# w_down in two transfers of 2 MB, and an up projection on interleaved pairs of columns

## What is computed

```
logits = v @ w_router + b_router            # 32 experts, the best 4 for each token
for each expert e, with the tokens that chose it:
    h   = x @ w_up[e] + b_up[e]             # 1024 -> 2048
    glu = min(h[:, :1024], 7)
    lin = clip(h[:, 1024:], -7, 7)
    act = glu * sigmoid(1.702 * glu) * (lin + 1)
    y   = act @ w_down[e] + b_down[e]       # 1024 -> 1024
f = sum over a token's 4 experts of gate * y
```

## Time and profile before

| | |
|---|---|
| three timed runs | 1293.08, 1294.69, 1295.81 us; median 1294.69 |
| the profiled execution | 1289.3 us, of which the span (first to last instruction) is 1287.5 |
| TensorE busy | 1198.5 us, 93% of the span |
| w_up matmuls (L909) | 2240 instructions, 504.7 us busy, mean 596 ns |
| w_down matmuls (L943) | 1120 instructions, 250.7 us busy, mean 601 ns |
| VectorE, ScalarE, GpSimd busy | 44%, 20%, 12% |
| SyncE's DMA queue | 52809 packets, 460.11 MB, 87.0% of 16 engines' span |
| chain that ended last | 63% TensorE, 26% transfers, 8% VectorE |

### The profile page before, as it was taken

How to read it: one execution, slowest core, us unless ns; L and a number is a source line. 1 busy time by engine, 2 the same in 40 slices (tenths; PEclk the granted TensorE clock), 3 DMA queues, 4 the chain that set the end, 5 groups by cost and what they waited for, 6 DMA issues and landing times.

```text
span 1287.5 us, 17057 instructions
## 1 busy us (share of the span) xinstructions
PE 1198.5 (93%) x5960; PEld 517.8 (40%) x5961; DVE 563.7 (44%) x1059; ACT 255.8 (20%) x404; POOL 160.7 (12%) x96
## 2 busy tenths in 40 slices
PE   5999999979999999899999999999999999999991
PEld 2688885523333333333333333333333333333330
DVE  0507815774443443344433444433444434434457
ACT  1523210242112111111112111212111211111121
POOL 0556462045200000000000000000000000000024
PEclk9999999989999999999999999999999999999995
DMA  9966696469999999999987999997999999699961
GB/s 334 349 248 263 247 301 227 145 257 419 406 427 427 427 426 426 425 426 426 428 379 300 427 425 428 426 428 303 377 427 427 428 426 426 262 424 426 427 252 41
DMA packets 54780, 466.33 MB, mean 362 GB/s; under 512 B 5511, under 2 KB 5671, under 8 KB 18633
## 3 DMA queue, kind: packets, MB, share of 16 engines
q1 hardware_dynamic: 52809, 460.11, 87.0%
q0 software_dynamic: 1952, 5.97, 1.4%
HBM read 464.29 MB, written 1.77 MB: 362 GB/s over the span
## 4 chain that ended last, share of the span: by engine, by line
PE 63%; DMA 26%; DVE 8%; ACT 1%; POOL 1%; issue 1%; SPq 0%; DVEq 0%; ACTq 0%; POOLq 0%
PE bank L909 26%; DMA ring<-in_w_up 24%; PE bank L943 12%; PE bank L695 8%; PE bank L885 3%; PE bank L746 3%; PE bank L763 2%; DMA ring<-in_w_ada 2%; PE bank L810 2%; PE bank L637 1%; PE bank L681 1%; PE bank L934 1%; DVE front L1407 1%; POOL front L547 1%; ACT front L1100 1%
## 5 line engine op out<-in xcount | busy, mean ns | idle before, releaser
L909 PE MATMUL bank<-ring,front 128*64 128x512 f32 x2240 | 504.7, 596 | 21.0 <-DMA ring<-in_w_up 21.0
L909 PEld LDWEIGHTS bank<-ring,front 128*64 128x64 f32 x2240 | 152.8, 137 | 314.4 <-issue 268.8
L943 PE MATMUL bank<-ring,front 128*64 128x512 f32 x1120 | 250.7, 601 | 6.8 <-ACT front L1100 6.8
L1380 DVE TENSOR_TENSOR front<-front,bank 128x512 f32<-128x512 f32 (+1 forms) x210 | 143.9, 685 | 56.8 <-PE bank L885 35.1
L1366 DVE TENSOR_TENSOR O_parts<-bank,O_parts 64x512 fp32r<-64x512 f32 x70 | 48.2, 689 | 239.2 <-ACT O_parts L1066 234.7
L943 PEld LDWEIGHTS bank<-ring,front 128*64 128x64 f32 x1120 | 77.9, 138 | 155.8 <-issue 142.0
L1097 ACT ACTIVATE front<-front 128x256 f32<-128x256 f32 x70 | 29.2, 417 | 504.3 <-DVE front L1398 504.3
L579 POOL TENSOR_TENSOR parts_home<-front 128x1024 f32<-128x1024 f32 (+1 forms) x2 | 5.2, 2576 | 917.8 <-DVE onehot_T L1421 917.8
L1398 DVE TENSOR_SCALAR front<-bank 128x256 f32<-128x256 f32 x70 | 29.7, 425 | 163.7 <-PE bank L909 162.5
L885 PE MATMUL bank<-O_parts,onehot_T 128*128 128x512 f32 x216 | 81.3, 454 | 11.2 <-DVE front L1446 6.5
L1066 ACT ACTIVATE O_parts<-bank 64x512 fp32r<-64x512 f32 x70 | 41.4, 591 | 237.5 <-PE bank L943 236.7
(11 more groups left out here) (217 smaller groups left out, 871.5 us busy)
## 6 DMA issues: line engine op xcount, KB each, us to landing
ring<-in_w_up SPq DMA_DIRECT2D x128, 2048.0 KB, 18.2
ring<-in_w_down SPq DMA_DIRECT2D x128, 1024.0 KB, 17.5
ring<-in_w_ada SPq DMA_DIRECT2D x12, 2048.0 KB, 11.9
ring<-in_w_in SPq DMA_DIRECT2D x7, 2048.0 KB, 8.0
ring<-in_w_o SPq DMA_DIRECT2D x2, 2048.0 KB, 21.0
hx<-in_x_prompt SPq DMA_DIRECT2D x2, 1024.0 KB, 8.2
ring<-in_w_in SPq DMA_DIRECT2D x4, 512.0 KB, 22.3
ring<-in_w_out_a SPq DMA_DIRECT2D x1, 2048.0 KB, 7.6
```

What stands on the lines that cost most here:

```text
L909: last = mm(bank[B_UP[j]][64 * h:64 * h + 64, :], x_T[:, (c % 2) * 2 + b, 64 * (c // 2):64 * (c // 2) + 64], w[:, :, at:at + 256], start=F ...
L943: last = mm(bank[B_DOWN][64 * h:64 * h + 64, :], act_T[:, 2 * j + b, 64 * hh:64 * hh + 64], expert_chunk_at(UP_CHUNKS + m)[:, b * 1024 + h ...
L1380: signal(TT(Y[0:r, 2 * t + h, :], Y[0:r, 2 * t + h, :], bank[b][0:r, :], ALU.add), bank_free[b], value)
```

## The change

w_down comes in two transfers of 2 MB, one for each slot (`DOWN_CHUNKS` 2): four rows of w_down to a partition, 16 KB in one run. Slot j then has row j*512 + 4p + b at place b of partition p, b from 0 to 3. So that `act_T` still meets the right rows, the up projection hands its columns out in another way: half h of group j now has the columns j*512 + 4q + 2h + {0, 1}, q from 0 to 127, for glu and for lin. The new function `columns` selects them, for the weights and for the bias: two neighbours, a gap of two, two neighbours. VectorE's and ScalarE's code stays as it is.

```diff
-UP_CHUNKS, DOWN_CHUNKS = 4, 4
+UP_CHUNKS, DOWN_CHUNKS = 4, 2
 
         def expert_chunk_at(c):
-            if c < UP_CHUNKS:
-                return ring[:, EXPERT_SLOT[c], :]
-            s, half = divmod(c - UP_CHUNKS, 2)
-            return ring[:, EXPERT_SLOT[UP_CHUNKS + s], half * 2048:(half + 1) * 2048]
+            return ring[:, EXPERT_SLOT[c], :]
...
+            def columns(row, j, h):
+                return row.rearrange("p (g j q b) -> p g j q b", g=2, j=2, b=4)[:, :, j, :, 2 * h:2 * h + 2]
...
                     for h in range(2):
-                        at = j * 512 + h * 256
-                        mm(bank[b][64 * h:64 * h + 64, :], up_sel[:, 0:SLOTS],
-                           b_up_parts.rearrange("p (g m) -> p g m", g=2)[:, :, at:at + 256], start=True, stop=False)
+                        mm(bank[b][64 * h:64 * h + 64, :], up_sel[:, 0:SLOTS], columns(b_up_parts, j, h), start=True, stop=False)
...
-                    w = expert_chunk_at(c)[:, b * 2048:(b + 1) * 2048].rearrange("p (g m) -> p g m", g=2)
+                    w = expert_chunk_at(c)[:, b * 2048:(b + 1) * 2048]
                     for h in range(2):
-                        at = j * 512 + h * 256
                         last = mm(bank[B_UP[j]][64 * h:64 * h + 64, :], x_T[:, (c % 2) * 2 + b, 64 * (c // 2):64 * (c // 2) + 64],
-                                  w[:, :, at:at + 256], start=False, stop=c == UP_CHUNKS - 1 and b == 1)
+                                  columns(w, j, h), start=False, stop=c == UP_CHUNKS - 1 and b == 1)
...
-                for m in range(DOWN_CHUNKS):
-                    j, hh = divmod(m, 2)
-                    pe.wait_ge(expert_landed[UP_CHUNKS + m], e * 16 + 16)
-                    for b in range(2):
+                for j in range(DOWN_CHUNKS):
+                    pe.wait_ge(expert_landed[UP_CHUNKS + j], e * 16 + 16)
+                    for b in range(4):
+                        hh = b // 2
                         for h in range(2):
-                            last = mm(bank[B_DOWN][64 * h:64 * h + 64, :], act_T[:, 2 * j + b, 64 * hh:64 * hh + 64],
-                                      expert_chunk_at(UP_CHUNKS + m)[:, b * 1024 + h * 512:b * 1024 + (h + 1) * 512],
-                                      start=m == 0 and b == 0, stop=m == DOWN_CHUNKS - 1 and b == 1)
-                    if m < DOWN_CHUNKS - 1:
-                        last.then_inc(expert_used[UP_CHUNKS + m], 1)
+                            last = mm(bank[B_DOWN][64 * h:64 * h + 64, :], act_T[:, 2 * j + b % 2, 64 * hh:64 * hh + 64],
+                                      expert_chunk_at(UP_CHUNKS + j)[:, b * 1024 + h * 512:b * 1024 + (h + 1) * 512],
+                                      start=j == 0 and b == 0, stop=j == DOWN_CHUNKS - 1 and b == 3)
+                    if j < DOWN_CHUNKS - 1:
+                        last.then_inc(expert_used[UP_CHUNKS + j], 1)
```

More of the change, by code:

```diff
@@ L470, in _ @@
             for c in range(EXPERT_CHUNKS):
-                s = EXPERT_SLOT[c if c < UP_CHUNKS else UP_CHUNKS + (c - UP_CHUNKS) // 2]
+                s = EXPERT_SLOT[c]
                 if s in ROW_SLOT:
```

## The result

| | before | after |
|---|---|---|
| median of the timed runs, us | 1293.08 (7 runs, 1291.88 to 1295.81) | 1298.96 (7 runs, 1296.66 to 1300.84) |
| ratio after/before | | 1.0042, 95% interval 1.0033 to 1.0052 |
| profiled execution, us (span) | 1289.3 (1287.5) | 1300.84 (1299.0) |
| a round that waits for nothing, us | 27.05 | 27.70 |
| a round paced by the transfers, us | 29.52 | 29.37 |

The change costs 5.9 us between the medians, 0.42% by the ratio, where a gain of 4.2 us was forecast (from a base of 1294.7 us, the median of three runs; that of all seven is 1.6 us lower). The profiled execution of after is the slowest of its seven, so sums are made between medians, or inside the loop over the experts.

The account below looks back on a forecast made before the run. TensorE and the weight transfers were both taken as near full, transfers setting the end of three stretches and TensorE the rest. 1294.7 - 4.2 us for longer runs, nothing for hand-over or columns, gave 1290.5 us; range 1287.5 to 1312.

Parts of the forecast that it names:

- Part 3: Up projection and bias matmuls reading interleaved pairs of columns: taken to cost nothing, bounded from 0 to +6.9 us a round.
- break-even, 0.39: Extra time per round, 0.39 us, from which a slower up projection read would cancel the 4.1 us gained by faster transfers.
- Rival P2: Up projection's moving read held up at each change of line: +24 us at d = 1.4 us a round; chance 0.22.
- The second reason given for 0: Up projection read: pairs make one step in two elements, L819 one in each, so the extra cost was taken as nothing.
- The rule weighed there: SBUF reads: two hits per 16-byte line suffice for full bandwidth; pairs give exactly two, so the interleaved read is free.
- Part 1: w_down transfers: rows of 16 KB instead of 8 KB move like w_up, saving 0.175 us an expert, 4.2 us in all.
- all of it is gained: In the expert loop, all 4.2 us count because each stretch waits longer than its share: 18.5, 3.5 and 3.0 us.
- the second and the third stretch: Expert-loop spans from a queue restart to TensorE's last wait, with 3.5 and 3.0 us of waiting to absorb slower rounds.
- Part 2: w_down slots handed over in 2 MB wholes, issued 1.72 us later: no cost, at most 0.2 us in the first round.
- the second and the third restart: Where the weight queue starts again after running dry; its lead is shortest there, but 2 MB transfers were expected to cost nothing.
- the margin of 1.4 us: After a queue restart: w_down's first 2 MB lands at 711.7 behind w_up, against 710.3 from an empty queue.
- The formula for a slower round: Extra d us a round: paid fully in 6.5 rounds outside stretches; inside, it first uses up waits of 16.4, 2.4, 1.9 us.

Follow-up runs that it names:

- e7: The changed kernel with each up projection matmul cut into two of 256 columns, pairs of columns kept: 1300.73 us, one run.
- e8: The changed kernel with each up projection matmul cut into two of 256 columns, each read as one run of 256: 1289.51 us, one run.
- e4: The changed kernel, but the up projection reads every second column instead of pairs, act_T's rows matching: 1298.18 us, ratio to before 1.0037.
- e10: The changed kernel, but each up projection matmul reads one float of every four, over all 2048 columns: 1797.76 us, one run.
- e3: The changed kernel with contiguous columns in runs of 256, w_down's two 2 MB transfers gathered from two 8 KB runs a partition: 1294.54 us, ratio to before 1.0006.
- e2: The kernel before, keeping its four 1 MB transfers, with only the interleaved pairs of columns added: 1300.61 us, ratio to before 1.0059.
- e1: The changed kernel's two 2 MB transfers with 16 KB runs kept, but columns read in runs of 256: 1290.12 us, ratio to before 0.9978.
- e5: The changed kernel, but the up projection reads four neighbouring columns and skips four, filling pieces of 16 bytes: 1289.91 us, one run.
- e6: The changed kernel with pairs, but TensorE's two halves read different groups of 512 columns: 1298.78 us, one run.
- e9: The changed kernel, but the up projection reads four neighbours of each eight, lying across a 16-byte border: 1298.2 us, one run.

## Why the prediction was wrong

**Part 3 failed, in its size: the price of the interleaved read, taken at nothing, is 0.65 us a round.** The prediction named the moving read as the unknown, bounded it from 0 to 6.9 us a round, and took 0; it measured 0.65. Its break-even, 0.39, lies between, so the sign turned. Rival P2, at 0.22, is what happened, near its mild end: d = 0.65 in place of the 1.4 that was priced at +24 us. The step that failed is the choice of the value. It had two rows to choose from: the matmuls of L819 with 283 against 273 ns, 3.7% longer, and its weight loads with 207 against 140, 48% longer. It went by the matmuls, which was the better of the two (592 to 612 ns is 3.4%), and then took their 10 ns as the price of an instruction whatever its columns. But L819's matmuls have 128 columns and L909's 512, and e7 and e8 show that the price goes with the columns. Taken as a share, 3.7% of 14.4 us is d = 0.53, beyond the break-even, and the forecast would have been slower. Even that was read off a row in which the strided operand is the weight, not the moving one; it came near, which is no proof that the two have one cause.

The second reason given for 0, that a pair of neighbours is one step in two columns where L819 has one in each, fell by e4: every second column costs what pairs cost.

The rule weighed there was read by half. The Trainium skill ("SBUF — State Buffer", Specifications (TRN2)) says that two hits on a line of 16 bytes are wanted for full bandwidth, and in the same place that each step to a new line pays a penalty. The runs bear out the penalty, with a size that the page doesn't give: at two hits the additional lines still cost 0.18 us of 3.65. The two hits they bear out in float32, where one hit halves the pace (7.40 us a chunk in e10), but not in bf16, where two hits a line take 631 ns against 379.

**Part 1 was right in its mechanism and nearly in its size.** w_down in runs of 16 KB moves at w_up's rate, because of the runs (e3) and not of the number of transfers; the saving is 0.155 us an expert, 0.175 was forecast, so 3.7 us and not 4.2. What it could not keep is the argument that all of it is gained: with rounds of 27.70 us there is nothing to wait for in the second and the third stretch (12 of the 24 experts), so that there a faster transfer changes nothing more. e2 has no waiting rounds there either. Beside the pairs only the first stretch's 12 x 0.155 = 1.9 us are gained; the ratios of after and e2, 1.0042 and 1.0059, differ by 2.2 us, though their intervals overlap.

**Part 2 was taken at nothing, and this nearly holds.** In after the second and the third restart lose 0.1 and 0.4 us, and no round of the stretches behind them waits. But the margin of 1.4 us on which it rested is not safe: e1 lost 1.1 and e3 1.3 and 1.9 us at places where the same working promises none. On the side of TensorE nothing appeared: L941 waits for ScalarE as L943 did, not for w_down.

**The formula for a slower round was right.** With the measured d it gives +7.5 for e2 (7.6 measured) and +5.6 for after (5.9 measured). Only 6.5 rounds and the two short stretches pay; the first stretch hides its 8.8 us in waits for w_up.

## What to carry to other kernels

A kernel in which two resources share the bound by stages gains from one of them only as long as the other keeps its pace: here a layout made for the DMA was paid for by the engine that reads it, and keeping long runs on both sides (e1) had both. Before a moving operand is read with gaps, count the pieces of 16 bytes that it touches, in the bytes of its own type, and place the gaps so that whole pieces are read. A price taken over from a row of another shape must be scaled by what it depends on; where that isn't known, work it out both ways, per instruction and per column, and see whether the sign hangs on it.

## What the runs showed of the hardware

- TensorE's moving read of float32 with 512 columns: 592 ns where every touched piece of 16 bytes is read whole, with or without gaps between (e1, e5); 612 ns where half of each is read, in whatever pattern (after, e4, e6, e9); 1079 ns where a quarter is read (e10). In bf16: 379 ns whole (before), 388 half (after, e5), 631 a quarter (e10).
- Alignment alone can cost it: four neighbours of each eight take 592 ns where they begin on a border of 16 bytes (e5) and 612 ns where they lie across one (e9).
- The queue of weights moves 420 to 423 GB/s with runs of 8 KB and 426 to 434 with 16 KB, for transfers of 2 MB with either (e3, after).
- After a restart a transfer of 2 MB that is issued some 3 to 3.8 us ahead of the landing before it may land up to 1.9 us later than a full queue would have it (w_down in after, e1 and e3, w_up in before); w_down's transfers of 1 MB, issued 5.0 to 6.0 us ahead, did not (4.96 to 4.98 us in before and e2). The cause is open.
